# Hybrid encoder layer: rotary tables behind the convolutions, final norm in column halves, another order of the latent projections

## The reference

```python
h = rmsnorm(x, norm_mix)
proj = h @ w_in        # c_q, c_kv, k_rope, dq, dk, dv, dz, da, db, mq, gate_logits
cos, sin = rope_tables(positions)              # positions * inv_freq
q = (rmsnorm(c_q) @ w_uq); kv = (rmsnorm(c_kv) @ w_ukv)      # 8 heads, rotary on 32 columns
o_mla = softmax(q k^T * 96**-0.5) v
qkv = silu(short_conv([dq, dk, dv]))           # 5 taps, along the tokens
q, k = l2norm(q), l2norm(k)                    # per head of 64
o_dn = gated delta rule in both directions, chunked, then norm, gain and silu(dz)
o_mem = softmax(mq mk^T) mv                    # mk, mv from rmsnorm(mem) @ mem_w_kv, 256 tokens
x = x + (sigmoid gates * (o_b @ w_branch_b), summed over b) @ w_out
h = rmsnorm(x, norm_ffn)
x = x + (silu(g) * u) @ w_down                 # g, u = h @ w_gate_up, 2816 wide
out = rmsnorm(x, final_norm)
```

## Time and profile before

| | us |
|---|---|
| median of 3 runs (lowest, highest) | 1099.53 (1098.12, 1100.18) |
| profiled execution | 1097.38 |
| its span, first to last instruction | 1095.7 |
| TensorE busy in it | 1048.0 (96%) |
| mean granted TensorE clock | 0.986 of full |

### The profile page before, as it was taken

One profiled execution on the slowest core, in us unless ns is written; L12 is line 12 of the kernel. 1 busy time (PEld: TensorE's weight loads), 2 busy tenths in 40 slices (PEclk: granted clock), 3 DMA queues, 4 the chain that ended last, 5 costly groups with the idle time before them and its releaser, 6 DMA issues.

```text
span 1095.7 us, 14406 instructions
## 1 busy us (share of the span) xinstructions
PE 1048.0 (96%) x5926; PEld 871.4 (80%) x5926; DVE 527.6 (48%) x745; ACT 378.2 (35%) x563; POOL 124.1 (11%) x199
## 2 busy tenths in 40 slices
PE   8899999989988998999999999989999999999995
PEld 7789798756678887877888888878888888888884
DVE  5774445566757687354342515462324232322314
ACT  5454644755432212333322222242323232311212
POOL 4000000625852341000000000000000000000000
PEclk9999999999999999999999999999999999999998
DMA  9313220000100013114142326314242423233201
GB/s 300 114 48 116 91 92 1 1 1 11 16 14 2 1 40 116 39 39 131 61 133 77 99 77 230 104 51 115 78 115 77 115 77 115 77 116 113 93 6 77
DMA packets 104000, 87.18 MB, mean 80 GB/s; under 512 B 13109, under 2 KB 93697, under 8 KB 103936
## 3 DMA queue, kind: packets, MB, share of 16 engines
q1 hardware_dynamic: 102288, 81.80, 24.8%
q0 software_dynamic: 1488, 4.40, 1.1%
q10 hardware_dynamic: 160, 0.07, 0.0%
HBM read 83.64 MB, written 2.62 MB: 79 GB/s over the span
## 4 chain that ended last, share of the span: by engine, by line
PE 84%; DVE 8%; issue 3%; ACT 2%; POOL 2%; DMA 1%; SPq 0%; DVEq 0%; POOLq 0%; ACTq 0%
PE psum L891 23%; PE psum L892 22%; PE psum L893 22%; PE psum L1196 2%; PE psum L1203 1%; PE psum L1216 1%; PE psum L1339 1%; PE psum L1268 1%; PE psum L1170 1%; PE psum L1295 1%; PE psum L1325 1%; PE psum L1351 1%; PE psum L1019 1%; POOL Zs L800 1%; DMA x_tok<-in_x_dram 1%
## 5 line engine op out<-in xcount | busy, mean ns | idle before, releaser
L891 PE MATMUL psum<-hT_hi,w_hi 128*128 128x512 f32 (+1 forms) x712 | 280.5, 394 | 7.4 <-DVE w_lo L1950 5.6
L892 PE MATMUL psum<-hT_lo,w_hi 128*128 128x512 f32 (+1 forms) x712 | 278.9, 392 | 0.0
L893 PE MATMUL psum<-hT_hi,w_lo 128*128 128x512 f32 (+1 forms) x712 | 278.7, 391 | 0.0
L1950 DVE TENSOR_TENSOR w_lo<-w_raw,w_hi 128x2048 fp32r<-128x2048 f32 (+2 forms) x81 | 167.5, 2068 | 230.9 <-ACT w_hi L1508 230.9
L1508 ACT ACTIVATE w_hi<-w_raw 128x2048 fp32r<-128x2048 f32 (+2 forms) x82 | 141.4, 1724 | 163.9 <-PE psum L893 151.6
L891 PEld LDWEIGHTS psum<-hT_hi,w_hi 128*128 128x128 f32 (+1 forms) x712 | 134.6, 189 | 37.8 <-DVE w_lo L1950 7.0
L893 PEld LDWEIGHTS psum<-hT_hi,w_lo 128*128 128x128 f32 (+1 forms) x712 | 134.3, 189 | 28.9
L892 PEld LDWEIGHTS psum<-hT_lo,w_hi 128*128 128x128 f32 (+1 forms) x712 | 134.4, 189 | 28.0
L1950 DVE TENSOR_TENSOR psum<-gate_act,psum 128x512 f32<-128x512 f32 x22 | 15.3, 696 | 119.6 <-PE psum L893 119.6
L891 PE MATMUL psum<-w_hi,act_hi 128*128 128x512 f32 x176 | 68.5, 389 | 0.0
L892 PE MATMUL psum<-w_lo,act_hi 128*128 128x512 f32 x176 | 68.5, 389 | 0.0
(11 more groups left out here) (308 smaller groups left out, 1570.5 us busy)
## 6 DMA issues: line engine op xcount, KB each, us to landing
w_raw<-in_w_in_dram SPq DMA_DIRECT2D x23, 1024.0 KB
w_raw<-in_ffn_w_gate_up_dram SPq DMA_DIRECT2D x44, 512.0 KB
w_raw<-in_ffn_w_down_dram SPq DMA_DIRECT2D x10, 1024.0 KB
w_raw<-in_mem_w_kv_dram SPq DMA_DIRECT2D x4, 1024.0 KB
w_raw<-in_w_out_dram SPq DMA_DIRECT2D x4, 1024.0 KB
x_tok<-in_x_dram SPq DMA_DIRECT2D x4, 512.0 KB, 5.2
w_raw<-in_w_branch_mla_dram SPq DMA_DIRECT2D x4, 512.0 KB
w_raw<-in_w_branch_dn_dram SPq DMA_DIRECT2D x4, 512.0 KB
```

The source lines that it names most:

```text
L891: pe.matmul(o, s_hi, m_hi, start=first, stop=False)
L892: pe.matmul(o, s_hi, m_lo, start=False, stop=False)
L893: return pe.matmul(o, s_lo, m_hi, start=False, stop=last)
L1950: return dve.tensor_tensor(o, a, b, op)
```

## The change

Three places, edited at once.

1. **Rotary tables.** VectorE's angles become the function `rope_angles`, called behind the memory splits of `c` 0; the mask copy moves into block 3 of the convolution loop; ScalarE's two Sin calls move behind the memory splits of `c` 1, ahead of `prep(("mq", 0))`. Their scratch `rope_t` moves, as its old place is written by then.
2. **Final norm.** The squares of columns 0 to 511 are summed while the second half's product runs, those of 512 to 1023 after it; both are scaled so that the sum is the mean. GpSimd multiplies x1 by the weights as each half tile is ready. The roots are made for two tiles at a time. ScalarE scales tiles 0 and 1, VectorE tiles 2 and 3, and SyncE stores in the order 0, 2, 1, 3.
3. **Latent projections.** ScalarE's `prep(("ukv", 0))` comes ahead of the last memory output. VectorE sums the squares, and makes their means, ahead of the gates' rows; the root stays behind them. The v tiles are turned in pairs after `up_kv` 2 and 3 instead of four behind all, and VectorE copies them in pairs at t = 2 and 3. ScalarE loads the exponential table behind the last key copies instead of ahead of them.

```diff
@@ -183,8 +183,9 @@
         turn(("kvA", t), low)
         turn(("kvB", t), low)
         heads("qT" if t < 2 else "kT", (t + 2) % NT)
-    for t in range(NT):
-        turn(("tok", t, 2), high)
+        if t >= 2:
+            for u in (2 * t - 4, 2 * t - 3):
+                turn(("tok", u, 2), high)
...
                     at_col += c
             ot = out[0].rearrange("(t p) d -> t p d", p=P)
-            for t in range(NT):
-                sp.wait_ge(y_ready, t + 1)
+            for t in (0, 2, 1, 3):
+                sp.wait_ge(y_ready[t], 1)
                 sp.dma_start(ot[t], y_out[:, t, :]).then_inc(out_stored, 16)
...
             consumed(pool, index[("gu", NF - 1)])
             pool.dma_start(fin_w[:, :], final_norm.partition_broadcast(P)).then_inc(fin_landed, 16)
+            pool.wait_ge(fin_landed, 16)
+            for half in range(2):
+                c = slice(512 * half, 512 * half + 512)
+                for t in range(NT):
+                    pool.wait_ge(x2_ready, NT * half + t + 1)
+                    pool.tensor_tensor(y_out[:, t, c], x1[:, t, c], fin_w[:, c], ALU.mult).then_inc(xw_ready, 1)
...
                     head_T("kT", t - 2, k_placed)
-            for t in range(NT):
-                to_tokens(t, 2)
+                    for u in (2 * t - 4, 2 * t - 3):
+                        to_tokens(u, 2)
             head_T("kT", 2, k_placed)
...
@@ -1578,11 +1587,6 @@
             filled(act, ("vec2",))
             A(vcol[:, V_MEM:NV], bank(("vec2",), P, NV)[:, V_MEM:NV]).then_inc(free(("vec2",)), 1)
             released(act, ("vec2",))
-
-            act.wait_ge(rope_in, 1)
-            w = NT * ROPE // 2
-            A(sin[:, :, :].rearrange("p t w -> p (t w)"), rope_t[:, 0, :], ACT.Sin).then_inc(rope_ready, 1)
-            A(cos[:, :, :].rearrange("p t w -> p (t w)"), rope_t[:, 1, :], ACT.Sin).then_inc(rope_ready, 1)
...
                     A(dnT[:, CT - 1, :], dnT[:, CT - 1, :], ACT.Silu).then_inc(dnT_ready, 1)
                 for k in range(4 * cb, 4 * cb + 4):
                     split_T(("memT", k), memT_hi[:, k, :], V_MEM + k, MEM)
+            act.wait_ge(rope_in, 1)
+            w = NT * ROPE // 2
+            A(sin[:, :, :].rearrange("p t w -> p (t w)"), rope_t[:, 0, :], ACT.Sin).then_inc(rope_ready, 1)
+            A(cos[:, :, :].rearrange("p t w -> p (t w)"), rope_t[:, 1, :], ACT.Sin).then_inc(rope_ready, 1)
             prep(("mq", 0))
...
             attention("mem", MH, NM, 0, oT_mem, memory_values)
+            prep(("ukv", 0))
             out_T("mem", NT - 1, oT_mem)
-            prep(("ukv", 0))
...
 
             for k in range(2):
                 turned_normed(k)
+            heads_T("kT", kT, 3, kT_ready)
             exp_tables()
-            heads_T("kT", kT, 3, kT_ready)
...
                 A(act_hi[:, f, :], bank(("u", f))).then_inc(glu_hi, 1)
+            def final_squares(half, t):
+                act.wait_ge(x2_ready, NT * half + t + 1)
+                squares(x1[:, t, 512 * half:512 * half + 512], square4[:, 512 * half:512 * half + 512],
+                        small[:, 0, NT * half + t:NT * half + t + 1], D ** -0.5)
+
+            def final_scale(t):
+                A(y_out[:, t, :], y_out[:, t, :], scale=rstd[:, t:t + 1]).then_inc(y_ready[t], 1)
+
             for half in range(2):
                 for f0 in range(0, NF, 4):
                     prep(after(("down", half, f0)))
+                    if half == 1 and f0 == 4:
+                        for t in range(NT):
+                            final_squares(0, t)
             root_tables()
             for t in range(NT):
-                act.wait_ge(x2_ready, NT + t + 1)
-                squares(x1[:, t, :], square4[:, :], small[:, 0, t:t + 1])
-                root("final", small[:, 2, t:t + 1], small[:, 1, t:t + 1], t)
+                final_squares(1, t)
+                if t == 2:
+                    root("final", small[:, 2, 0:2], small[:, 1, 0:2], 0)
+            root("final", small[:, 2, 2:4], small[:, 1, 2:4], 1)
+            act.wait_ge(rstd_final, 1)
+            act.wait_ge(xw_ready, NT + 2)
+            for t in range(2):
+                final_scale(t)
...
@@ -2019,29 +2043,12 @@
             dve.wait_ge(w_lo_done, 1)
             prep(("dn", 1))
 
-            dve.wait_ge(consts_landed, 16 * 10)
-            dve.tensor_copy(masks[:, :, :], table_in[:, :, :]).then_inc(consts_ready, 1)
-
-            link(dve.tensor_copy(pos_f[:, :], pos_i[:, :]))
-            w = ROPE // 2
...
             for i in range(6):
                 if i > 0:
                     prep(after(("dn", i)))
+                if i == 3:
+                    dve.wait_ge(consts_landed, 16 * 10)
+                    dve.tensor_copy(masks[:, :, :], table_in[:, :, :]).then_inc(consts_ready, 1)
...
+            def rope_angles():
+                link(dve.tensor_copy(pos_f[:, :], pos_i[:, :]))
+                w = ROPE // 2
+                ang, turns, half_turn = rope_t[:, 0, :], rope_t[:, 1, :], rope_t[:, 2, :]
...
                 prep(after(("c", cb)))
                 for k in range(4 * cb, 4 * cb + 4):
                     split_T(KD + k, ("memT", k), memT_hi[:, k, :], memT_lo[:, k, :], V_MEM + k, MEM)
+                if cb == 0:
+                    rope_angles()
             released(dve, ("c", 1, NT - 1))
...
             prep(("ukv", 0))
+            for t in range(NT):
+                for pt in range(2):
+                    n = 2 * t + pt
+                    released(dve, ("tok", t, pt))
+                    dve.tensor_reduce(small[:, 0, pt * 32 + t * 8:pt * 32 + t * 8 + 8],
+                                      square2[:, n % 2, :].rearrange("p (h n) -> p h n", n=DK), AX.X,
+                                      ALU.add).then_inc(sq_ready, 1)
+            dve.wait_ge(sq_ready, 2 * NT)
+            mean_squares(slice(0, 64), 1.0)
             dve.wait_ge(gc_ready, 2)
             filled(dve, ("mem", "oT", NT - 1))
...
             dve.wait_ge(nb_ready, 1)
             tt(neg_bexp[:, :], neg_beta[:, :], dg[:, 4, :], ALU.mult).then_inc(rowq_ready, 1)
-            for t in range(NT):
-                for pt in range(2):
-                    n = 2 * t + pt
-                    released(dve, ("tok", t, pt))
-                    dve.tensor_reduce(small[:, 0, pt * 32 + t * 8:pt * 32 + t * 8 + 8],
-                                      square2[:, n % 2, :].rearrange("p (h n) -> p h n", n=DK), AX.X,
-                                      ALU.add).then_inc(sq_ready, 1)
-            dve.wait_ge(sq_ready, 2 * NT)
-            rsqrt("qk", slice(0, 64), 1.0, rstd[:, :])
+            rsqrt("qk", slice(0, 64), 1.0, rstd[:, :], begun=True)
             dve.tensor_scalar(rstd[:, 0:32], rstd[:, 0:32], DK ** -0.5, None, ALU.mult).then_inc(rstd_dn, 1)
...
                 dve.tensor_copy(dst[:, :, NOPE:QK], kr).then_inc(k_placed, 1)
-                if t == 2:
-                    filled(dve, ("kvB", NT - 1))
-                    for u in range(NT):
-                        key = ("tok", u, 2)
-                        filled(dve, key)
-                        dve.tensor_copy(v_tok[:, u, :], bank(key)).then_inc(free(key), 1)
+                for u in (2 * t - 4, 2 * t - 3) if t >= 2 else ():
+                    key = ("tok", u, 2)
+                    filled(dve, key)
+                    if u == 0:
+                        filled(dve, ("kvB", NT - 1))
+                    dve.tensor_copy(v_tok[:, u, :], bank(key)).then_inc(free(key), 1)
...
                 for t in range(NT if half == 0 else 1):
                     add_glu(half, t)
-            dve.wait_ge(fin_landed, 16)
-            for t in range(NT):
-                if t + 1 < NT:
-                    add_glu(1, t + 1)
-                dve.wait_ge(ssq_ready, 2 * NT + NM + t + 1)
-                rsqrt("final", slice(t, t + 1), D, rstd[:, t:t + 1], t)
-                dve.scalar_tensor_tensor(out=y_out[:, t, :], in0=x1[:, t, :], scalar=rstd[:, t:t + 1], in1=fin_w[:, :],
-                                         op0=ALU.mult, op1=ALU.mult).then_inc(y_ready, 1)
+            def final_means(b):
+                dve.wait_ge(ssq_ready, 3 * NT + NM + 2 * b + 2)
+                dve.scalar_tensor_tensor(out=small[:, 1, 2 * b:2 * b + 2], in0=small[:, 0, 2 * b:2 * b + 2], scalar=EPS,
+                                         in1=small[:, 0, NT + 2 * b:NT + 2 * b + 2], op0=ALU.add, op1=ALU.add).then_inc(ms_ready, 1)
+
+            add_glu(1, 1)
+            add_glu(1, 2)
+            final_means(0)
+            add_glu(1, 3)
+            root_of("final", slice(0, 2), rstd[:, 0:2], 0, rstd_final)
+            final_means(1)
+            root_of("final", slice(2, 4), rstd[:, 2:4], 1, rstd_final)
+            dve.wait_ge(rstd_final, 2)
+            dve.wait_ge(xw_ready, 2 * NT)
+            for t in (2, 3):
+                dve.tensor_scalar(y_out[:, t, :], y_out[:, t, :], rstd[:, t:t + 1], None, ALU.mult).then_inc(y_ready[t], 1)
```

(45 more changed lines are left out.)

## The result

| | before | after |
|---|---|---|
| median of the runs, us | 1099.16 (1098.12 to 1100.18, 4 runs) | 1085.97 (1084.40 to 1086.66, 4 runs) |
| profiled execution, us | 1097.38 | 1086.66 |
| its span, us, and mean granted clock | 1095.7, 0.986 | 1084.9, 0.988 |
| TensorE's last matmul ends | 1083.0 | 1073.9 |
| from there to the end of the span | 12.7 | 11.0 |

The ratio of the times is 0.9889, with a 95% interval of 0.9871 to 0.9907: 13.2 us by the medians, 10.7 us between the two profiled executions. I had said 8.2 us and 1091.3, and 1088.6 for the low end of the range. The direction was right and the size was not.

A forecast was written before the change was run, and what follows sets the result against it. TensorE was taken to bound the kernel, busy 1048.0 of 1095.7 us. Gains 5.0 - 1.6 + 2.2 + 2.6 = 8.2 took 1097.38 to 1089.2 profiled, with 2.15 added 1091.3 median; range 1088.6 to 1095.3.

The forecast's parts named there:

- First place: Rotary chains leave the start: the 3.28 us wait at ("dn", 2) and the half-clock stretch behind it go, gain 5.0.
- Second place: Sine and cosine directly before w_hi of ("mq", 0), where there is no slack, delay TensorE by 1.6 us.
- Latent part: Reordered latent projections: 1.1 from the query side plus 1.1 from the key side, gain 2.2 us (0.2 to 3.3).
- now the row preparation of 3.0 us stands between: Between VectorE's last reduction and the root: delays the first kvA copy, so TensorE waits and keeps only 1.1 us.
- this half: Query side of the latent projections: the 2.3 us wait on square goes, net gain 1.1 us, bounds 0.5 and 1.7.
- key half: Last keys and exponential table before the first latent scores: gain 1.1 us, bounds -0.3 and 1.6.
- Final norm: Behind TensorE's last matmul: arithmetic ends 4.9 us earlier, but four queued stores leave a gain of 2.6 us.
- rivals 2 and 3: Final stores: not bound by the DMA engines, 1089.0, chance 0.10; or queueing with their whole latency, 1095.3, chance 0.06.
- rival 4: New hole at 117 us throws the clock down in the projections: slower, 1103 at 24 us half clock; chance 0.04.
- rival 1: Clock still falls near the start or behind 117 us, latent gain only 0.2: total 4.5, 1095.0; chance 0.14.

The follow-up runs named there:

- undo_squares: The kernel after, with VectorE's reductions of the query squares back behind the row preparation: 1086.82 us, one run.
- no_port: The kernel after, with VectorE instead of GpSimd multiplying weight and root into the last two half tiles in one pass: 1084.65 us.
- undo_whi: The kernel after, with ScalarE's prep(("ukv", 0)) back behind the last memory output: 1084.11 us, one run.
- latent_only: The kernel before, with only the reordered latent projections of the change: 1091.68 us, ratio 0.9943 to before.
- final_only: The kernel before, with only the final norm in column halves: 1096.15 us, ratio 0.9981 to before.
- sin_reload: The kernel after, with a load of the root's table ahead of the sine, so the sine's must be loaded again: 1087.26 us.
- rope_only: The kernel before, with only the rotary part of the change: 1092.40 us, ratio 0.9953 to before.
- silu_first: The kernel before, with one dummy Silu ahead of the sine while ScalarE waits for the angles: 1095.53 us, ratio 0.9972.
- undo_exp: The kernel after, with the exponential table loaded ahead of the last kT copies again: 1088.65 us, one run.
- tail_pairs_again: Repeat of the kernel after with VectorE multiplying the last two half tiles and the first tile pair finished and stored early: 1081.89 us, ratio 0.9861.

## Why the prediction was wrong, step by step

- **First place, +5.0: right.** No wait at `("dn", 2)` and no low clock there; its `w_lo` ends at 33.64, where I had 33.8.
- **Second place, -1.6: mis-sized, 0.3 measured.** I took the 1.60 us of the earlier trace rows, of which 1.28 are the load. Which table lies there depends on what ran before, and there Silu had run. In the kernel before, the sine's load was followed by another for Silu at 33.33, so I took the two to have different tables; no row showed the opposite order, in which Silu's table serves both. The page of the Trainium skill that I weighed (ScalarE: Activation LUTs, section What ACT_TABLE_LOAD costs) prices a load; the question was whether there would be one.
- **Latent part, +2.2: mis-sized, 4.0 measured.** The step that failed is "now the row preparation of 3.0 us stands between": in its new place it takes 1.7, since GpSimd's rotations are nearly over (the last one that lies beside it starts at 200.26), and that time is hidden behind ScalarE's root, as `undo_squares` shows. My upper bound of 1.7 for this half was too low as well; TensorE kept all of the 2.6 us on `square` and 0.2 on `qk_tok` behind it, and the half gave 2.95. The key half came out right (1.1 forecast, 1.0 measured), but in part by luck: the table was worth more and the order of turns less than nothing.
- **Final norm, +2.6: 1.7 measured.** The bound by the DMA engines and its 1.31 us per store were right, and rivals 2 and 3 fell. The step that failed is that the roots would be done at 1085.2: the second pair's root ends 3.0 us behind the last matmul, not 2.2. I gave VectorE's small products the length that they had with GpSimd idle; beside GpSimd two of them took 1.45 us instead of 0.36, and `no_port` gives the 1.1 us back.
- **The sum.** By the profiles the three errors are +1.7 (of which 1.3 are the sine), +1.8 and -0.9, which makes 10.8 from 8.2. The other 0.4 of the front lies in the first place: hole and clock together were worth 5.4, not 5.0.
- **The median, another 2.5.** I added a fixed 2.15 to get from a profiled execution to the median. The profiled execution of before (1097.38) is faster than its four other runs, that of after (1086.66) the slowest of its four. Over all runs on record the change measures 12.1 and not 13.2, so part of the miss is which runs fell into the first four. TensorE's clock is what varies: from the first latent score to the last matmul, the same instructions took 856.55 us before and 856.49 after, but 853.36 in `undo_whi` and 853.33 in `latent_only`, where 6.8 us at 0.50 lie in between instead of 17.0. So a low stretch there costs 0.31 us per us, where rival 4 reckoned t/2.

What stays open: why the mean clock rose as far as from 0.9857 to 0.9897. Two parts can be read off: the low stretch at the front that is gone (3.4 us, 0.0016) and the shorter half clock behind the last matmul (0.0007). For the remaining 0.0017 no run shows a cause. The fourteen profiles hold the same later holes, and the grant doesn't answer to them alike. This wait stands in each of them, here in the changed kernel:

```profile
PE psum L1334 <- DVE attT L1974: 3.3, 1, 3.3
...
424.00:431.00 7.00, 5.36 (x21) 4.97 (x22) 6.86 (x12) 1.91 (x1) 0.00 (x0) 0.56 0.44 146
```

In all fourteen the grant fell in or just behind it, for 3.4 us in seven and for 6.8 in seven, and it fell at the earlier holes of 3.2 to 3.4 us of before, `latent_only`, `final_only` and `sin_reload` as well. At the 2.3 us wait on `w_lo` (486.5 in the changed kernel) it fell in six of the fourteen. Of the other holes of 2.3 to 2.6 us it fell at those of `rope_only` at 194, `silu_first` at 40 and `undo_exp` at 219, and not at those of before, `final_only` and `silu_first` at 198 to 199. In `tail_pairs_again` it fell at 225.4 with no wait over 0.8 us in the 20 us ahead. So the grant fell at each of these holes of over 3 us, and at a shorter one now and then; which of two runs of one kernel gets more low stretches, no run here settles. My rival 1 bet on the clock giving less, and none on its giving more: that side of the range was missing.

## What to carry to other kernels

Before a step that needs a table is priced with its load, look which table its engine will hold in the new place. Before a step is priced by its row, look what ran on GpSimd beside it, in the old place and in the new. And where the runs of one kernel scatter with the granted clock by more than the edit is worth (here from 1094.3 to 1100.7 us), compare the landmarks of the traces first. Time x clock is the coarser tool: it counts a low stretch at more than it costs, also where TensorE has no work. Let the range reach to both sides by that scatter.

## What the runs showed of the hardware

- Whether sine and Silu share a table depends on their order: sine first took two loads of 1.28 us (30.46 and 33.33 in the kernel before), Silu first took one (`silu_first`, and the changed kernel at 93.55).
- Small VectorE operations are stretched while GpSimd works on tensors: 1.45 against 0.36 us for two 128x2 products, 0.44 to 0.51 against 0.18 for some of the 128x32 ones. One that falls between two rotations isn't: in the kernel before, the one at 196.42 took 0.17, with rotations to 196.46 and from 196.53. The stretch goes both ways. GpSimd's first rotation in the kernel before, beside a `w_lo` of VectorE, against a later one:

```profile
193.46 1.72 POOL L714 TENSOR_TENSOR rope_x<-qk_tok,cos 128x128 f32<-128x128 f32 x1 [67.88 <-ACT qk_tok L1508]
...
196.00 0.46 POOL L716 TENSOR_TENSOR rope_x<-qk_tok,cos 128x128 f32<-128x128 f32 x1
```

The Trainium skill (SBUF — State Buffer, section SBUF: two separate sides) says that VectorE and GpSimd share one pair of ports as "an **exclusive lock**, not a bandwidth split", also for VectorE operations with two inputs in SBUF. The traces here agree for the products (1.45 against 0.36 us), and I hadn't applied it to the rows at 194.78 to 197.77.
- Four stores of 512 KB issued within 2.9 us move at 393 to 410 GB/s together, and their landing takes 2.7 to 4.8 us from issue, against 2.6 for a lone one.
